# Two rounded matmul passes for the square sums of 22 single queries and keys, and the rotary products behind the scores' maximum

## What is computed

```python
def rms_norm(x, w):
    y = x32 * lax.rsqrt(jnp.mean(x32 * x32, axis=-1, keepdims=True) + EPS)
    return (y * w).astype(x.dtype)

def diff_attention(q_raw, k_raw, v_raw, q_norm_w, k_norm_w, lam_params, subln_w, lambda_init, cos, sin):
    q = rms_norm(q_raw.reshape(b, l, A_HEADS, 2, A_QK_DIM), q_norm_w)
    k = rms_norm(k_raw.reshape(b, l, A_HEADS, 2, A_QK_DIM), k_norm_w)
    q = jnp.concatenate([apply_rope(q[..., :A_ROT], c, s), q[..., A_ROT:]], axis=-1)
    ...
    p = softmax32(jnp.einsum('bqhmd,bkhmd->bhmqk', qb, k), scale)
    w = (p[:, :, 0] - lam * p[:, :, 1]).astype(v.dtype)
    o = rms_norm(o, subln_w) * (1.0 - lambda_init)

def latent_attention(...):
    q_rope = apply_rope(rms_norm(q[..., C_NOPE:], q_norm_w[C_NOPE:]), cos[:, None, :], sin[:, None, :])
    k_rope = apply_rope(rms_norm(kr_raw, k_norm_w[C_NOPE:]), cos, sin)

x = x + jnp.einsum('bln,nd->bld', y, w_out)
```

## Time and profile before

| what | value |
|---|---|
| median of 3 runs | 905.96 us (905.85 to 906.21) |
| the profiled execution, its time | 905.9 us |
| its span, first to last instruction | 904.1 us |
| busy: PE, DVE, ACT | 896.1, 639.3, 566.3 us |
| granted TensorE clock | 1.0 throughout (the 2.4 GHz level) |
| DMA, mean busy share per slice | 0.2 to 0.8 |

### The profile page before, as it was taken

One profiled execution on the slowest core, in us unless ns is written; L12 is line 12 of the kernel. 1 busy time (PEld: TensorE's weight loads), 2 busy tenths in 40 slices (PEclk: granted clock), 3 DMA queues, 4 the chain that ended last, 5 costly groups with the idle time before them and its releaser, 6 DMA issues.

```text
span 904.1 us, 18068 instructions
## 1 busy us (share of the span) xinstructions
PE 896.1 (99%) x7070; PEld 860.1 (95%) x7070; DVE 639.3 (71%) x1073; ACT 566.3 (63%) x985; POOL 0.2 (0%) x4
## 2 busy tenths in 40 slices
PE   8999999999999999999999999999999999999998
PEld 7999998998999999999999999999999999999998
DVE  7785987779777776766665659876787667766552
ACT  7678756577666667745554588556676666665331
POOL 0000000000000000000000000000000000000000
PEclk9999999999999999999999999999999999999999
DMA  8754433333434343444455553344324444445562
GB/s 333 264 197 142 150 129 131 123 139 113 149 138 146 134 156 121 154 144 188 169 199 186 187 181 146 126 136 160 140 98 183 140 141 159 150 159 187 187 211 70
DMA packets 22996, 143.83 MB, mean 159 GB/s; under 512 B 2560, under 2 KB 4736, under 8 KB 6528
## 3 DMA queue, kind: packets, MB, share of 16 engines
q1 hardware_dynamic: 22768, 142.64, 43.7%
q10 hardware_dynamic: 144, 0.04, 0.0%
HBM read 140.58 MB, written 2.10 MB: 158 GB/s over the span
## 4 chain that ended last, share of the span: by engine, by line
PE 94%; ACT 3%; DVE 2%; DMA 1%; issue 0%; SPq 0%; ACTq 0%; DVEq 0%
PE dense L733 26%; PE dense L735 25%; PE dense L734 25%; PE s_ps L902 4%; PE o_ps L938 4%; PE norm_ps L857 2%; PE t_ps L917 2%; ACT w_hi L1028 1%; DVE w_lo L1331 1%; DMA x<-xt_dram 1%; PE swap_ps L881 0%; ACT h_hi L1009 0%; PE swap_ps L735 0%; PE norm_ps L735 0%; PE norm_ps L734 0%
## 5 line engine op out<-in xcount | busy, mean ns | idle before, releaser
L733 PE MATMUL dense<-h_hi,w_hi 128*128 128x272 f32 (+2 forms) x1440 | 427.2, 297 | 1.9 <-DVE h_lo L1311 1.8
L735 PE MATMUL dense<-h_hi,w_lo 128*128 128x272 f32 (+2 forms) x1440 | 412.8, 287 | 0.0
L734 PE MATMUL dense<-h_lo,w_hi 128*128 128x272 f32 (+2 forms) x1440 | 411.0, 285 | 0.0
L1331 DVE TENSOR_TENSOR w_lo<-raw,w_hi 128x1024 fp32r<-128x1024 f32 (+1 forms) x257 | 313.3, 1219 | 87.3 <-ACT w_hi L1028 80.5
L1028 ACT ACTIVATE w_hi<-raw 128x1024 fp32r<-128x1024 f32 (+1 forms) x257 | 271.4, 1056 | 70.8 <-PE dense L735 56.1
L733 PEld LDWEIGHTS dense<-h_hi,w_hi 128*128 128x128 f32 x1440 | 271.4, 188 | 7.4 <-issue 3.0
L734 PEld LDWEIGHTS dense<-h_lo,w_hi 128*128 128x128 f32 x1440 | 271.5, 189 | 1.2
L735 PEld LDWEIGHTS dense<-h_hi,w_lo 128*128 128x128 f32 x1440 | 271.2, 188 | 0.0
L733 PE MATMUL dense<-y_hi,w_hi 128*128 128x272 f32 (+1 forms) x500 | 143.6, 287 | 0.5 <-DVE w_lo L1331 0.3
L735 PE MATMUL dense<-y_hi,w_lo 128*128 128x272 f32 (+1 forms) x500 | 142.7, 285 | 0.0
L734 PE MATMUL dense<-y_lo,w_hi 128*128 128x272 f32 (+1 forms) x500 | 142.4, 285 | 0.0
(11 more groups left out here) (173 smaller groups left out, 805.7 us busy)
## 6 DMA issues: line engine op xcount, KB each, us to landing
raw<-w_stream_dram SPq DMA_DIRECT2D x128, 1024.0 KB, 4.8
out_dram<-x SPq DMA_DIRECT2D x8, 256.0 KB, 5.9
x<-xt_dram SPq DMA_DIRECT2D x3, 544.0 KB, 8.9
raw<-w_stream_dram SPq DMA_DIRECT2D x3, 512.0 KB, 7.6
con<-consts_dram SPq DMA_DIRECT2D x1, 984.0 KB, 8.2
x<-xt_dram SPq DMA_DIRECT2D x2, 272.0 KB, 4.8
raw<-w_stream_dram SPq DMA_DIRECT2D x2, 256.0 KB, 4.5
d_w<-consts_dram SPq DMA_DIRECT2D x2, 256.0 KB, 5.5
```

Of the source, the lines that this page charges most:

```text
L733: nc.tensor.matmul(ps, whi, xhi, start=first, stop=False)
L734: nc.tensor.matmul(ps, whi, xlo, start=False, stop=False)
L735: return nc.tensor.matmul(ps, wlo, xhi, start=False, stop=last)
L1331: signal(nc.vector.tensor_tensor(w_lo[:, g % RING, 0:n], raw[:, e % RAW, CHUNK * half:CHUNK * half + n], w_hi[:, g % RING, 0:n].bitcast(F3 ...
```

## The change

Three things are changed.

1. The sums of the 22 single queries and keys are no longer one full fp32 matmul. ACT writes, behind the squares, a rounded copy of them (`sq_hi`, type fp32r); DVE writes the remainder (`sq_lo`, the new step `sq_low`); and TensorE multiplies a rounded copy of `halves` (`sums_of`, made once) with each of the two, accumulating. So each sum has one more ACT instruction and one more DVE instruction, and `rope_stat` waits for DVE (`summed`) rather than for ACT (`pre_done`). The paired queries and keys keep their sums.
2. For branch A (`aq`, `ak`; 16 of the 22), `rope_stat` and `rope_fin` stand a slot later. `sub_slot` follows: the slots that the A heads' norms keep clear of are now `pair_slot + 5` and `+ 6`, which moves four of the eight `sub_stat`: three in the first layer one slot later, into slots that have scores, and one in the second layer two slots earlier.
3. The rotary products of single queries and keys (`rope_turn`, before `single_mid`) stand at 0.65 of the slot in place of 0.25: behind `s_max`, `s_scale` and the new `sq_low`, and ahead of the split.

```diff
-AT_VECTOR = dict(sq_sum=0.2, rope_mid=0.25, s_max=-0.418, ...
+AT_VECTOR = dict(sq_sum=0.2, sq_low=0.6, rope_mid=0.25, rope_turn=0.65, s_max=-0.418, ...
@@ make_plan
                 if kind in ("aq", "ak"):
                     at(s, ("rope_pre", l, kind, i0 + j, j))
-                    at(s, ("rope_mid", l, kind, i0 + j))
-                    at(s, ("rope_stat", l, kind, i0 + j))
-                    at(s + 1, ("rope_fin", l, kind, i0 + j))
+                    at(s, ("rope_turn", l, kind, i0 + j))
+                    at(s, ("sq_low", "rope", l, kind, i0 + j))
+                    at(s + 1, ("rope_stat", l, kind, i0 + j))
+                    at(s + 2, ("rope_fin", l, kind, i0 + j))
...
         at(s + 9, ("rope_pre", l, "kr", 0, None))
-        at(s + 10, ("rope_mid", l, "kr", 0))
+        at(s + 9, ("sq_low", "rope", l, "kr", 0))
+        at(s + 10, ("rope_turn", l, "kr", 0))
...
             else:
-                at(s + 1, ("rope_mid", l, key, i))
+                at(s, ("sq_low", "rope", l, key, i))
+                at(s + 1, ("rope_turn", l, key, i))
@@ sub_slot
-            taken |= {pair_slot(p) + 4, pair_slot(p) + 5}
+            taken |= {pair_slot(p) + 5, pair_slot(p) + 6}
@@ tensor, rope_stat
             t0 = rope_from(l, key)
+            pe.wait_ge(summed, sum_no[("rope", l, key, i)])
+            norm_free("rope_stat", l, key, i)
+            half = parity("rope_stat", l, key, i)
             if key in PAIRED:
-                pe.wait_ge(summed, sum_no[("rope", l, key, i)])
+                sums = nc.tensor.matmul(norm_ps[:, t0:L], halves, sq[:, 2 * half, t0:L], start=True, stop=True)
             else:
-                pe.wait_ge(pre_done, pre_no[("rope_pre", l, key, i)])
...
+                nc.tensor.matmul(norm_ps[:, t0:L], sums_of[:, :], sq_hi[:, half, t0:L], start=True, stop=False)
+                sums = nc.tensor.matmul(norm_ps[:, t0:L], sums_of[:, :], sq_lo[:, half, t0:L], start=False, stop=True)
@@ scalar, rope_pre
-            signal(nc.scalar.activation(sq[:, 2 * half, t0:L], rope_source(key, i)[:, t0:L], ACT.Square), pre_done,
+            link(nc.scalar.activation(sq[:, 2 * half, t0:L], rope_source(key, i)[:, t0:L], ACT.Square))
+            signal(nc.scalar.activation(sq_hi[:, half, t0:L], sq[:, 2 * half, t0:L], ACT.Copy), pre_done,
                    pre_no[("rope_pre", l, key, i)])
@@ vector, new
+        def sq_low(what, l, key, i):
+            t0, half = rope_from(l, key), parity("rope_stat", l, key, i)
+            dve.wait_ge(pre_done, pre_no[("rope_pre", l, key, i)])
+            signal(nc.vector.tensor_tensor(sq_lo[:, half, t0:L], sq[:, 2 * half, t0:L],
+                                           sq_hi[:, half, t0:L].bitcast(F32), ALU.subtract), summed,
+                   sum_no[(what, l, key, i)])
```

More of the change, by code:

```diff
@@ L131 @@
                  lift=0.6, up_out=0.705, up_next=0.715, split=0.71, x_square=0.72, y_gate=0.73, y_lat=0.74, lam_exp=0.793, v_out=1.297)
-AT_VECTOR = dict(sq_sum=0.2, rope_mid=0.25, s_max=-0.418, lam_dot=-0.35, sub_fin=-0.345, rope_fin=-0.34, lat_fin=0.055, head_out=0.17,
+AT_VECTOR = dict(sq_sum=0.2, sq_low=0.6, rope_mid=0.25, rope_turn=0.65, s_max=-0.418, lam_dot=-0.35, sub_fin=-0.345, rope_fin=-0.34, lat_fin=0.055, head_out=0.17,
                  y_split=0.75, pool=0.266, xscale=0.283, gate=0.7, s_scale=0.491, x_out=0.512, rescale=0.55,
@@ L298, in build @@
     sq = sb("sq", [128, 4, L])
+    sums_of = sb("sums_of", [128, 128], F32R)
+    sq_hi = sb("sq_hi", [128, 2, L], F32R)
+    sq_lo = sb("sq_lo", [128, 2, L], F32R)
     rn = sb("rn", [128, L])
@@ L395, in build @@
     lam_ready, lam_exp = sem("lam_ready"), sem("lam_exp")
+    ones_ready = sem("ones_ready")
     tails_zero = sem("tails_zero")
@@ L503, in build @@
             scaled_no[stg[1:]] = len(scaled_no) + 1
-        if stg[0] == "sq_sum":
+        if stg[0] in ("sq_sum", "sq_low"):
             sum_no[stg[1:]] = len(sum_no) + 1
-        if stg[0] == "rope_mid":
+        if stg[0] in ("rope_mid", "rope_turn"):
             mid_no[stg[1:]] = len(mid_no) + 1
@@ L851, in rope_stat @@
             t0 = rope_from(l, key)
+            pe.wait_ge(summed, sum_no[("rope", l, key, i)])
+            norm_free("rope_stat", l, key, i)
+            half = parity("rope_stat", l, key, i)
             if key in PAIRED:
-                pe.wait_ge(summed, sum_no[("rope", l, key, i)])
+                sums = nc.tensor.matmul(norm_ps[:, t0:L], halves, sq[:, 2 * half, t0:L], start=True, stop=True)
             else:
-                pe.wait_ge(pre_done, pre_no[("rope_pre", l, key, i)])
-            norm_free("rope_stat", l, key, i)
-            sums = nc.tensor.matmul(norm_ps[:, t0:L], halves, sq[:, 2 * parity("rope_stat", l, key, i), t0:L],
-                                    start=True, stop=True)
+                if (l, key) == (0, "kr"):
+                    pe.wait_ge(ones_ready, 1)
+                nc.tensor.matmul(norm_ps[:, t0:L], sums_of[:, :], sq_hi[:, half, t0:L], start=True, stop=False)
+                sums = nc.tensor.matmul(norm_ps[:, t0:L], sums_of[:, :], sq_lo[:, half, t0:L], start=False, stop=True)
             sums.then_inc(stat_done, 1)
@@ L999, in lambda_exp @@
             signal(nc.scalar.activation(lam_sum[:, :], lam_sum[:, :], ACT.Exp), lam_exp, 1)
+            act.wait_ge(s_const, 16)
+            nc.scalar.activation(sums_of[:, :], halves, ACT.Copy).then_inc(ones_ready, 1)
         def x_tile(l, kt):
@@ L1357, in sq_sum, with rope_turn @@
             signal(nc.vector.tensor_tensor(a, a, b, ALU.add), summed, n)
-        def single_mid(l, key, i):
+        def sq_low(what, l, key, i):
[4 more added lines that the diff above has]
+                   sum_no[(what, l, key, i)])
+        def rope_turn(l, key, i):
             branch, t0 = rope[key][0], rope_from(l, key)
@@ L1378, in rope_mid @@
         def rope_mid(l, key, i):
-            if key not in PAIRED:
-                single_mid(l, key, i)
-                return
             t0 = rope_from(l, key)
@@ L1514, in _ @@
         run = dict(setup=setup, split_half=split_half, x_half=x_half, x_first=x_first, x_add=x_add, lam_dot=lam_dot, lam_out=lam_out,
-                   x_out=x_out, split=split, rescale=rescale, sq_sum=sq_sum, rope_mid=rope_mid, rope_fin=rope_fin,
+                   x_out=x_out, split=split, rescale=rescale, sq_sum=sq_sum, sq_low=sq_low, rope_mid=rope_mid, rope_turn=rope_turn, rope_fin=rope_fin,
                    lat_fin=lat_fin, sub_fin=sub_fin, head_out=head_out, y_split=y_split, gate=gate, pool=pool,
@@ L1519, in _ @@
         for stage, *what in vector_plan:
-            if stage in ("rope_mid", "rope_fin") and not waited[0]:
+            if stage in ("rope_mid", "rope_turn", "rope_fin") and not waited[0]:
                 dve.wait_ge(s_tab, 16)
```

## The result

| what | before | after |
|---|---|---|
| median of 7 runs each, side by side | 905.99 us (905.85 to 906.21) | 908.77 us (907.18 to 909.19) |
| ratio, with 95% interval | | 1.0027 (1.0017 to 1.0037) |
| the profiled execution, its time and span | 905.9, 904.1 us | 907.24, 905.2 us |

The change makes the kernel slower by 0.27%, a little more than the 0.2% that I had called no change. The measured time is 2.2 us above the forecast of 906.6 and outside the forecast's own case of 904.1 to 907.8; it lies inside the whole range by 0.03 us. The executions of the changed kernel fall into two groups, and the median can't be understood without that: two of the seven have a mean granted TensorE clock of 1.0 and take 907.2 us, five have 0.998 and take 908.6 to 909.2. The profiled one belongs to the first group.

A forecast was written before the change was run, and what follows sets the result against it. TensorE, 99% busy, sets the end, with ACT or DVE nearly full in two stretches. First layer +0.7 and second +0.05, about +0.7 on 905.9, gave 906.6 us: 4.6 saved, 5.3 returned as waits; range 902.9 to 908.8.

The forecast's parts named there:

- the forecast's own case: Whole kernel: time within 0.2% of the forecast 906.6 us, 904.1 to 907.8; chance 0.52.
- TensorE's saving: At the 22 single sums: each costs 0.25 us instead of 0.46, saving 0.21, or 4.6 us in all.
- Rival 4: At the sums: rounded passes are not cheaper because type changes cost, no saving, 911.2 us; chance 0.03.
- Stretch 1: C norms, both layers: two ACT copies delay chunk 25's lift by 0.92 us; net +0.43 first layer, +0.50 second.
- The head product at slot 33: Second layer, behind the C norms: DVE's late `yt` makes TensorE's last transpose wait another 0.35 us.
- Stretch 2: A heads 2 and 3, first layer: DVE's weights come 1.4 us late for the transpose; net +1.15 us.
- Heads 0 and 1 of the second layer: Branch A: saving of 0.83 us less about 0.2 for a late head product, net -0.6.
- Heads 2 and 3 of the second layer: Branch A: saving 0.83, new waits of 0.6 and 0.5, the 0.47 wait at 674.83 goes; net -0.2 us.
- The clock: Whole kernel: no clock term; dense passes taken as 0.125 us apart throughout.
- rival 3: Pooling stretch, both layers: DVE's backlog is not taken up, up to 1.1 us more per layer, 908.8; chance 0.19.
- Rival 1: Whole kernel: side engines absorb all added work, all 4.6 us kept, 901.3 us; chance 0.12.
- Rival 2: One stretch's backlog smaller: 905.1 to 905.4, inside the forecast's 0.52; both smaller: 903.5 to 904, chance 0.14.

The follow-up runs named there:

- Experiment 1: Changed kernel with only the 6 sums of kr and qr rounded, the 16 A sums full fp32 at their old slots: 907.11 us, ratio 1.0013.
- experiment 6: Changed kernel, first-layer A key 3's rotary products moved behind the weights, qr 0's squares and copy behind the lifts in both layers: 905.69 us, ratio 0.9995.
- Experiment 3: Changed kernel with first-layer A key 3's rotary products 0.9 of a slot later, behind the weights of slot 59: 905.65 us, ratio 0.9997.
- experiment 9: Kernel before the change with only the single rotary products moved to 0.65 of the slot, sums full fp32 at old slots: 905.54 us, ratio 0.9996.
- experiment 2: Changed kernel with only the 16 branch A sums rounded and moved, kr and qr keeping full sums: 905.75 us, ratio 1.0003.
- experiment 7: The kernel of experiment 6 with second-layer A query 3's rotary products also 0.9 of a slot later: 905.74 us, ratio 0.9998.
- experiment 10: Changed kernel run again without an edit, to get a trace of a slower execution: 908.67 us, clock 0.998.

## Why the prediction was right, and where it was wrong

**TensorE's saving: right.** 0.21 per sum, and the neighbours lose nothing. Rival 4 falls. The Trainium skill ("FP8 and Floating Point Precision", TensorE Precision Notes) puts true FP32 at 4 passes, which would make the saving, as an estimate, 4 x 0.125 - 0.25 = 0.25; the two traces have 0.46 - 0.25 = 0.21, and the measurement decides.

**Stretch 1: right in size, incomplete in place.** The two copies ahead of the lift cost +0.93 in the first layer and +0.91 in the second, where the working had 0.85 and 0.92. (The working goes by chunk 25's second pass, which is 0.86 late in the first layer: 88.02 against 87.04, less the 0.12 by which this trace was late already. Half of its 0.88 would put the lift's end at 86.67, not 86.63; nothing hangs on that.) They don't all fall on chunk 25, though: +0.21 and +0.47 of it already fall on slot 24, where the paired sum waits for the inverse root (0.7 us longest, the row `norm_ps` <- `rn` of the waits). The prediction named only the lift. One queue of ACT stands behind both, so the sum is the same. Experiment 1 shows this half by itself, and experiment 6 shows why it isn't mended by another place in the table.

**The head product at slot 33: right.** DVE's product ends at 578.17 + 0.42, and the transpose starts behind it, as the two rows below (DVE, then TensorE) show; the earlier trace rows are the same place before. The step is +0.42 for the forecast 0.35.

```profile
578.17 0.42 DVE L1468 TENSOR_TENSOR yt<-o_ps,g_st 128x256 f32<-128x256 f32 x1
```

```profile
578.65 0.29 PE L931 MATMUL o_ps<-con,probs 128*32 128x128 f32 x1 [0.18 <-DVE yt L1468]
```

**Stretch 2: right, but for what comes behind the wait.** The weights end at 232.99 and the transpose starts at 233.05; the prediction had 233.3 and 233.36 on a clock from which TensorE was 0.26 early by then. The new pause before the maximum is 0.54 us in the trace, 0.6 in the sum. Net +1.10 for +1.15. Experiment 3 shows the cause: with the rotary products of one key out of that list the step is gone; experiment 9 shows that their place alone, without the remainders, doesn't make it.

**Heads 0 and 1 of the second layer: mis-sized.** The forecast was -0.83 + 0.2. The first two sums give their share; then TensorE loses 0.52 at 614.44 by the starts (0.36 of it shown as idle). The term looked on DVE for a late head product, and the wait is ACT's: the copy of the squares stands ahead of the copies of the transposed weights, which `pv` waits for. ACT's rows, and TensorE's under them:

```profile
613.03 0.43 ACT L1113 ACTIVATE sq_hi<-sq 128x272 fp32r<-128x272 f32 x1
613.49 0.60 ACT L1222 ACTIVATE p_t<-t_ps 128x512 f32<-128x512 f32 x1
614.12 0.27 ACT L1224 ACTIVATE p_t<-o_ps 32x128 f32<-32x128 f32 x1
```

```profile
614.44 1.60 PE L948 MATMUL o_ps<-p_t,v_st 128*128 128x128 f32 x12 [0.36 <-ACT p_t L1224]
```

Slot 49 gives another +0.26 when both halves of the change are in, and nothing with either alone (experiments 1 and 2): TensorE's chunk there starts 0.1 behind the first of two lifts that ACT does late; the cause of that one is read from the starts and not tested. Together the term was 0.64 too optimistic; the prediction listed ACT's copies at the `pv` of heads 2 and 3 of the same layer and did not look for them here. Small waits that went away elsewhere (-0.29 in the first layer at slot 107, -0.18 in the second at slot 36) bring the sum back to +1.1.

**Heads 2 and 3 of the second layer: right.** -0.26 for -0.2. The wait at 674.83 is gone, a step of -0.79 at slot 59, and those at slots 57 and 58 came (+0.32 and +0.12).

**The clock: the step that failed.** Every term was priced at the 2.4 GHz level, because the page showed 1.0 throughout, and the wait at slot 60 was counted by its length alone. In the runs it is followed by some 3.5 us at the lower level in 11 of the 19 executions of the changed kernel (5 of 7, 5 of 10, 1 of 2), which costs another 1.5. That moves the median from about 907.2, which the forecast's case would have held, to 908.8. No rival had it, and that 908.77 still lies in the range is luck: its upper end, 908.8, is the price of rival 3, a mechanism that did not occur (the pooling stretches show no new wait, and DVE's idle time of 0.58 at the earlier trace rows still stands at 0.42). The net at slot 60 was right to 0.05 us; what the working lacks is a price for what TensorE does after such a wait.

**The other rivals.** Rival 1, that the side engines absorb everything, falls with the first row of waits. The Trainium skill's rule ("Perfetto Trace Analysis", Identifying the Most-Contended Engine) is named there; for TensorE that section wants the share of the peak rate and the busy share of the weight loads in place of the matmuls' busy share; the weight loads' share is 95% in the earlier trace rows and still the highest, so TensorE would be the engine to relieve. Here relieving it by 4.6 us gave back all of it and 1.1 more. Rival 2 falls in both branches: both backlogs have their full size. Experiment 6 shows it from another side: where ACT is relieved ahead of the lift, the gain goes to a wait for DVE.

## What to carry to other kernels

When one engine is busy for 99% of the time and two others run without a pause in the same stretch, look at that stretch and not at the averages before you move work from the first to the others. Here the six sums of C made the kernel 1.2 us slower, the sixteen of A alone changed nothing (905.75), and the sixteen of A were worth 2.0 us (903.99) only once DVE's list ahead of the weights had been shortened. Where a full engine stands ahead of the one that sets the end, look first at what in its stream could go behind the result that is waited for: moving one key's rotary products was worth 1.6 us at clock 1.0 and 3.0 in the other executions. And don't price a wait like the one here by its length alone, nor judge it by one trace: the profiled execution, at clock 1.0, shows the wait but not the 1.5 us that follow it in 11 of 19 executions.

## What the runs showed of the hardware that was not expected

- The granted clock fell behind a TensorE wait of 1.52 us in about half of the executions: 11 of 19 of the changed kernel, 4 of 10 in experiment 2, which has the same wait. Behind 3.27 us it fell in 4 of 4 (by the mean clock; one of them has a trace). In the 60 executions of experiments 1, 3 and 6 to 9, whose longest waits past the program's first 12 us are 0.8 us or less, no mean is below 0.999. The one trace of these with 0.999 (experiment 7) has the lower level behind TensorE's last work, from 902.5 us on, where it costs nothing. The fall itself comes when TensorE has work again: in the trace of experiment 10 the granted clock reads 1.00 in the 2.2 us that hold the wait, and 0.52 in the 3.5 us behind it.
- What decides between the executions with the wait of 1.5 us is open. In two traces of the changed kernel, one of each kind, the steps of the slots from 24 to 61 agree within 0.02 us. They do differ at the program's start: the first passes (`s_ps` for `g_st`) start 0.45 us apart until 4.7 us, and then 0.23, in the trace with the fall, and 0.45 apart until 5.7 in the three traces without it. One trace against three is no proof.
- So TensorE begins the program at the lower level, and the 1.00 that the windows give for its first microseconds doesn't fit the pace of its passes. In the trace of experiment 2 the dense passes, too, start 0.23 us apart until 10.9 us, and 0.13 from then on, while its mean is given as 1.0. In the kernel before, the passes go from 0.45 to 0.22 at 4.7 us, and the "1.0 throughout" ahead of the prediction holds from there on.
- Nor is every longer wait followed by the fall. In the trace of the kernel before, TensorE stands 1.59 us for `h_lo` soon after that, and from the second pass behind it on the starts are 0.12 to 0.14 apart:

```profile
7.15 0.36 PE L733 MATMUL dense<-h_hi,w_hi 128*128 128x272 f32 x1 [1.59 <-DVE h_lo L1311]
7.35 0.28 PE L734 MATMUL dense<-h_lo,w_hi 128*128 128x272 f32 x1
7.47 0.30 PE L735 MATMUL dense<-h_hi,w_lo 128*128 128x272 f32 x1
7.61 0.29 PE L733 MATMUL dense<-h_hi,w_hi 128*128 128x272 f32 x1
```

- Two rounded passes between dense ones cost just what two dense passes cost, 0.125 us each at 272 columns, against 0.46 for the one full fp32 sum that they replace.
